# Eight pieces of a fused weight product put one by one in front of the forget-gate tiles, and a weight load moved behind the spreading of the reciprocals

## The chip, the cores and the metric

The kernel runs on one core of a Trainium2 chip. The metric is the device time of one execution in microseconds (us); before the change it is 2773.86 us, the median of 3 runs that lie between 2770.55 and 2777.31 us.

## The reference, cut to what matters

One decoder layer over 1024 tokens of width 1024, all in float32: two groups of 8 causal attention heads side by side (MLA, and FoX with a forget gate), an output projection, cross attention to 256 memory tokens with 4 heads, a mixture of 32 experts of which each token takes 4, and a last norm.

```
h = h + hybrid_mixer(rmsnorm(h, ln_mix), ...)
    # o_mla = causal_block_attention(q_mla, k_mla, v_mla, scale)
    # o_fox = causal_block_attention(fq, fk, fv, scale, c)   c: cumulative log forget gate,
    #         s = q @ k.T * scale + c[t] - c[s]; causal softmax; p @ v
    # return concat(rmsnorm(o_mla), rmsnorm(o_fox)) @ w_o
h = h + memory_cross_attention(rmsnorm(h, ln_cross), mem, ...)
    # k, v = split(rmsnorm(mem) @ w_mem_kv); p = softmax(q @ k.T * scale)
    # return concat over heads(p @ v) @ w_xo
h = h + moe_ffn(rmsnorm(h, ln_ffn), ...)
return rmsnorm(h, ln_final)
```

## The kernel before, in words

The program is written engine by engine: each engine has its own instruction list, run in the order in which it is written, and the lists meet at semaphores. The time has four big stages: projections (up to about 370 us), attention (370 to 705 us), cross attention and routing (to about 1130 us), experts (the rest). Only the attention stage is touched.

**The attention stage** runs over `HP` = 4 head pairs, called h = 0 to 3 here. The first three are iterations of a hardware loop, the fourth is written out behind it (`b_loop`). A head pair is two MLA heads and two FoX heads that share the row and column tiles. Inside one h there are `NP` = 16 positions p: p = 0 to 7 are the MLA tiles of 128 queries (y = 0), p = 8 to 15 the FoX tiles (y = 1, the "forget-gate pairs"). Tile i has 128·(i + 1) keys, and the order is `B_TILES = [6, 0, 7, 1, 5, 2, 4, 3]` in both halves, so p = 8 is tile 6, p = 9 tile 0, p = 10 tile 7, p = 11 tile 1, and so on. In each half every second tile is a short one (0, 1, 2, 3).

What happens to a tile, by engine and line:

- TensorE (PE) computes the scores into `wide[0]` and `wide[1]`, one for each of the two heads: `scores` (L1438) for MLA, `scores_pair` (L1455 and L1459) for FoX.
- VectorE (DVE) finds the lowest value of each row (L1950), for FoX it adds the forget-gate term first and puts the sum into `biased` (L1959).
- ScalarE (ACT) computes the exponential and the row sum (`b_exp`, L1109).
- PE turns the probabilities, 128 by 128 at a time (`turned`, L1312). DVE copies the first four blocks out of PSUM (L1970), ACT the rest (`b_second`, L1121).
- PE multiplies them with the values (`values`, L1494) into bank `pp[0]` or `pp[1]`, and ACT copies the result out (`b_out`, L1130).

PE works one tile ahead: at position p it turns tile p, computes the scores of tile p + 1, and multiplies the values of tile p - 1. At an odd FoX position the scores of p + 1 come first, at p = 8, 10, 12, 14 they come between the two heads' turns.

ACT's order at position p is `b_second(p, 0)`, `b_exp(p+1, 0)`, `b_second(p, 1)`, `b_exp(p+1, 1)`, `b_out(p-1)`, and then, where a head of the product below is complete, `mix_evict`.

**The fused product.** Beside the attention, each h computes a quarter (`MIX` = 256 columns) of (memory values) times `w_xo`, for the later cross attention. It is 8 pieces: 4 cross-attention heads `hd` by 2 blocks `mt` of 128 memory rows. A piece is `mixed(h, hd, mt, last)` (L1497 to L1507), two float32 products of 128x128 by 128x256; the trace shows a float32 product as two records of each kind. The two pieces of a head fill the two halves of one PSUM bank, `pp[1]`, which is the same bank that holds the values of p = 1, 3 and 5. So the first piece of each head waits until the bank is free, and the second tells ACT, which copies it out (`mix_evict`, L1142) and so frees it:

```
if mt == 0:
    pe.wait_ge(b_po[1].free, b_po[1].base + B_PO[1] * h + b_mix_use(hd))
    if hd == 0:
        pe.wait_ge(mix_in, mix_in_done + 16 * (h + 1))
```

`b_mix_use(hd)` counts the uses of the bank: 3 for values, then one per head. Hence the first piece of head 0 waits for `b_out(5)`, and that of head hd for `mix_evict(hd - 1)`. Where a piece stands is set by a table, `B_MIX`, whose rows are (position, hd, mt). PE puts the pieces of a position ahead of its turns:

```
if pair and y == 1 and not turn_first:
    scores_pair(*nxt)
for at_, hd, mt in B_MIX:
    if at_ == p:
        mixed(h, hd, mt, last)
for a_ in range(2):
    turned(h, p, a_)
```

`mix_evict(hd)` stands at the position of the second piece of its head.

**The loads and stores of the stage** are all issued by SyncE (SP) in one list for each h, `b_loads`: the MLA operands of the next h, the four stores of finished heads (`mix_store`, L661), the two spreads, the FoX operands of the next h (`load_fox`), and the next quarter of `w_xo` (`mix_load`, 1 MB into `mix_w`). A spread (`spread(h, y)`) takes the 16 rows of reciprocals of the softmax sums to a scratch tensor in HBM (`d_rr`, L676), waits for that store to land, and loads them back as `rr_all`, one row for 64 partitions. GpSimd (POOL) multiplies the output by it (`normalise`). For the last h, `mix_load` reads into `mix_w_last`, and the last third of `w_o` is loaded with it.

Of the kernel before, what the change touches and what calls it, by code (L numbers as in the profile page):

```python
# [78 lines left out]
def build(nc, S, a, out):  # L79
    T, D, NT, KD, H, FW, E, CAP = S.T, S.D, S.NT, S.KD, S.H, S.FW, S.E, S.CAP  # L80
    ctx = ExitStack()
    with ctx:
# [265 lines left out]

        B_MIX = [(NT + 2 * (n // S.MT), n // S.MT, n % S.MT) for n in range(S.XH * S.MT)]
        assert S.XH * S.MT * P == S.XH * S.M and B_MIX[-1][0] < NP - 1
        B_VALUES = [1 if p < NT - 1 and p % 2 else 0 for p in range(NP)]
        B_PO = [B_VALUES.count(0), B_VALUES.count(1) + S.XH]
# [219 lines left out]
        def rows(w):  # L574

            return w.rearrange("(k p) n -> p k n", p=P)
# [3 lines left out]
        def _(sp):  # L580
            def load(dst, src, s):
                sp.dma_start(dst, src).then_inc(s, 16)
# [64 lines left out]
            def load_mla(h):  # L647
                sp.wait_ge(b_in[0].free, h + 1)
                for dst, src in ((q_mla, d_q), (k_mla, d_k)):
                    load(dst[:, :, :], src[bass.ds(h * 2, 2), :, :].rearrange("h d t -> d h t"), b_in[0].full)  # L650

            def mix_load(h, last=False):
                if last:
                    sp.wait_ge(b_v, 2 * HP - 1)
                load(mix_w[last][:, :, :], rows(a["w_xo"][0])[:, :, bass.ds(h * MIX, MIX)], mix_in)

            def mix_store(h, hd, last=False):

                s = hd % 2
                sp.wait_ge(mix_full, mix_full_done + S.XH * h + hd + 1)  # L660
                sp.dma_start(d_vw[hd * S.M:(hd + 1) * S.M, bass.ds(h * MIX, MIX)].rearrange("(u m) n -> m u n", u=S.MT),  # L661
                             mix_out[last][s][:, :, :]).then_inc(mix_free[s], 16)

            def load_fox(h):
                sp.wait_ge(b_in[1].free, h + 1)
                for dst, src in ((q_fox, d_fq), (k_fox, d_fk)):
                    load(dst[:, :], src[bass.ds(h * P, P), :], b_in[1].full)
                sp.wait_ge(b_cneg.free, h + 1)
                for a_ in range(2):
                    load(cneg[a_][:, :], d_cneg[bass.ds(h * 2 + a_, 1), :].to_broadcast([P, T]), b_cneg.full)  # L670

            def spread(h, y):

                sp.wait_ge(b_row, 2 * h + y + 1)
                sp.wait_ge(b_all.free, 2 * h + y + 1)
                sp.dma_start(d_rr[y, :, :].rearrange("a (t p) -> (a t) p", p=P), rr_row[y][:, :]).then_inc(b_st, 16)  # L676
                sp.wait_ge(b_st, 16 * (2 * h + y + 1))
                for a_ in range(2):
                    load(rr_all[a_ * S.DV:(a_ + 1) * S.DV, :], d_rr[y, a_:a_ + 1, :].to_broadcast([S.DV, T]), b_all.full)
# [5 lines left out]
            def b_loads(h, last_mix):  # L685
                load_mla(h + 1)
                mix_store(h, 0)
                spread(h, 0)
                for hd in range(1, S.XH):
                    mix_store(h, hd)  # L690
                load_fox(h + 1)
                mix_load(h + 1, last_mix)
                if last_mix:
                    load(w_o[:, W_O_FIRST:, :], rows(a["w_o"][0])[:, W_O_FIRST:, :], ld["w_o"])
                spread(h, 1)

            with sp.Fori(0, HP - 2) as h:
                b_loads(h, False)
            b_loads(HP - 2, True)
            mix_store(HP - 1, 0, True)  # L700
            spread(HP - 1, 0)
# [312 lines left out]
        def _(ac):  # L1014
# [110 lines left out]
            def b_out(h, p):  # L1125

                (y, i), (b, use) = B_PAIRS[p], b_values_use(p)
                ac.wait_ge(b_po[b].full, b_po[b].base + B_PO[b] * h + use)
                apart(ac)
                ac.activation(o_t[:, bass.ds(h + y * HP, 1), i * P:(i + 1) * P].rearrange("p o t -> p (o t)"), pp[b][:, 0:P],  # L1130
                              ACT.Copy).then_inc(b_po[b].free, 1)
                ac.drain().then_inc(b_ot, 1)
# [13 lines left out]
            def b_body(h, last):  # L1146
                for p in range(NP):
# [5 lines left out]
                    if p:  # L1153
                        b_out(h, p - 1)
                    for at_, hd, mt in B_MIX:
                        if at_ == p and mt == S.MT - 1:
# [151 lines left out]
        def _(pe):  # L1308
# [134 lines left out]
            def scores_pair(h, p):  # L1443

                i = B_PAIRS[p][1]
                L = P * (i + 1)
                if p == NT:
                    pe.wait_ge(b_in[1].full, 32 * (h + 1))
                for a_ in range(2):
                    pe.wait_ge(b_s[a_].free, NP * h + p + 1)  # L1450
                half = [slice(a_ * S.DN, (a_ + 1) * S.DN) for a_ in range(2)]
                for c in range(0, L, 512):
                    w = min(512, L - c)
                    for a_ in range(2):
                        pe.matmul(wide[a_][:, c:c + w], q_fox[half[a_], i * P:(i + 1) * P], k_fox[half[a_], c:c + w],  # L1455
                                  start=True, stop=c + w < L)
                for idn, tri_mask, stop in ((ident_b, mask_b, False), (ident_x, mask_x, True)):
                    for a_ in range(2):
                        m = pe.matmul(wide[a_][:, L - P:L], idn[half[a_], :], tri_mask[half[a_], :], start=False, stop=stop)  # L1459
                        if stop:  # L1460
                            m.then_inc(b_s[a_].full, 1)
# [47 lines left out]
            def b_body(h, last):  # L1509
                for p in range(NP):  # L1510
# [4 lines left out]
# [4 lines that stand above are left out]
# [877 lines left out]
```

## Time and profile before

| what | value |
|---|---|
| time, median of 3 | 2773.86 us |
| the profiled execution's own time | 2772.76 us |
| its span in the profile | 2771.0 us |
| PE busy | 2663.8 us, 96% of the span |
| DVE, ACT, POOL busy | 39%, 23%, 14% of the span |
| mean granted TensorE clock | 0.986 |

The span is the stretch between the first and the last instruction of the profiled execution. In it PE is busy nearly all the time, and mostly in the experts. A busy share says nothing on one stage; for the attention stage it has to be read from that stretch.

### The profile page before, as it was taken

What the parts mean: (1) busy time and instruction counts of PE and PEld (TensorE: products, weight loads), DVE (VectorE), ACT (ScalarE), POOL (GpSimd) and SP (SyncE); (2) the same over time, 40 slices, a digit from 0 to 9 for tenths busy, and PEclk for the clock granted to TensorE, in tenths of its full rate; (3) what the DMA queues carried; (4) which work ended last, traced back from release to release, by engine and by line L of the source; (5) the groups of instructions that cost most, each with busy time, mean ns of one, the idle gap of its engine ahead of it and who ended that gap; (6) DMA issues with size and microseconds to landing.
All of it is one profiled execution on the core that took longest, in us unless ns stands there. A gap on an engine that the chain in (4) does not pass through costs nothing. (4 is left out here: it accounts for less than half of the span.)

```text
span 2771.0 us, 53372 instructions
## 1 busy us (share of the span) xinstructions
PE 2663.8 (96%) x19081; PEld 2288.0 (83%) x19082; DVE 1087.1 (39%) x2664; ACT 629.2 (23%) x1385; POOL 379.2 (14%) x390
## 2 busy tenths in 40 slices
PE   8999998899999999799999999999999999999997
PEld 7445556666458776699999999999999999999997
DVE  1111145455222323443333344344545454545454
ACT  0333344455001111011111111111212122121213
POOL 0000022112100000011111111111111111211112
PEclk9999999999999999899999999999999999999999
DMA  7111242322500000855666687787888888888785
GB/s 286 39 52 53 66 137 77 99 66 68 195 0 9 31 31 39 327 201 188 221 231 230 230 278 262 270 278 269 305 296 309 293 300 291 307 292 306 285 293 197
DMA packets 108867, 534.04 MB, mean 193 GB/s; under 512 B 24290, under 2 KB 59042, under 8 KB 84208
## 3 DMA queue, kind: packets, MB, share of 16 engines
q1 hardware_dynamic: 88016, 498.99, 49.2%
q0 software_dynamic: 20768, 33.97, 5.8%
q8 instruction: 49, 0.80, 0.1%
q14 instruction: 34, 0.28, 0.0%
HBM read 506.64 MB, written 60.52 MB: 205 GB/s over the span
## 5 line engine op out<-in xcount | busy, mean ns | idle before, releaser
L1319 PE MATMUL bank<-xe_t,slot 128*128 128x128 f32 (+4 forms) x8192 | 1022.4, 287 | 13.7 <-issue 12.5
L1319 PEld LDWEIGHTS bank<-xe_t,slot 128*128 128x128 f32 x8192 | 1013.0, 192 | 16.0 <-issue 15.9
L1734 PE MATMUL wide<-act_t,slot 128*128 128x128 f32 (+4 forms) x4096 | 513.3, 286 | 0.0
L1734 PEld LDWEIGHTS wide<-act_t,slot 128*128 128x128 f32 x4096 | 506.3, 191 | 0.0
L2235 DVE TENSOR_SCALAR glu<-bank,b_gu 128x256 f32<-128x256 f32 x256 | 123.9, 484 | 748.1 <-PE bank L1319 748.1
L1266 ACT ACTIVATE sig<-glu 128x256 f32<-128x256 f32 x256 | 106.6, 417 | 847.6 <-DVE glu L2235 844.0
L1373 PE MATMUL bank<-w_in,xt 128*128 128x512 f32 (+1 forms) x512 | 219.0, 581 | 3.8 <-DVEq L1878 3.8
L1277 ACT ACTIVATE y_t<-wide,b_dn 128x256 f32<-128x256 f32 x256 | 107.3, 470 | 427.4 <-PE wide L1734 427.4
L935 POOL DMA_INDIRECT xg<-d_xn,gidx x66 | 65.9, 999 | 900.9 <-DVEq L2194 890.9
L1373 PEld LDWEIGHTS bank<-w_in,xt 128*128 128x128 f32 x512 | 96.1, 193 | 104.1 <-issue 104.1
L948 POOL DMA_INDIRECT share<-d_gate,sidx x64 | 67.6, 1057 | 457.7 <-DVEq L2254 434.0
L2247 DVE TENSOR_TENSOR act_t<-lin,sig 128x256 f32<-128x256 f32 x256 | 108.9, 425 | 44.0 <-issue 11.2
L2237 DVE TENSOR_SCALAR lin<-bank,b_gu 128x256 f32<-128x256 f32 x256 | 121.7, 475 | 0.0
L1319 PEld LDWEIGHTS bank<-hn_t,w_xq 128*128 128x128 f32 x1024 | 115.5, 192 | 1.4 <-issue 1.1
L2244 DVE TENSOR_TENSOR lin<-lin,glu 128x256 f32<-128x256 f32 x256 | 108.8, 425 | 19.2
L1319 PE MATMUL bank<-hn_t,w_xq 128*128 128x128 f32 x1024 | 115.7, 275 | 0.3 <-issue 0.3
L1319 PE MATMUL wide<-vw,px_t 128*128 128x512 f32 x256 | 112.4, 593 | 0.6 <-DVE lg_now L2070 0.6
L1312 PE MATMUL bank<-const,prob 128*128 128x128 f32 x576 | 91.4, 288 | 21.6 <-ACT prob_t L1121 11.7
L958 POOL DMA_INDIRECT d_sum<-y_sb,sidx x62 | 100.7, 1624 | 39.1 <-ACTq L1247 24.2
L1837 DVE TENSOR_TENSOR xe_t<-bank,gains 128x512 f32<-128x512 f32 x132 | 85.3, 686 | 41.4 <-PE bank L1695 36.3
L1312 PEld LDWEIGHTS bank<-const,prob 128*128 128x128 f32 x576 | 64.4, 144 | 42.9 <-issue 15.6
L1970 DVE COPY prob_t<-bank 128x512 f32<-128x512 f32 (+3 forms) x128 | 75.7, 592 | 60.7 <-PE bank L1312 49.1
(282 smaller groups left out, 2321.2 us busy)
## 6 DMA issues: line engine op xcount, KB each, us to landing
slot<-in_w_gu SPq DMA_DIRECT2D x128, 2048.0 KB, 7.8
slot<-in_w_dn SPq DMA_DIRECT2D x64, 2048.0 KB, 7.7
w_in<-in_w_in SPq DMA_DIRECT2D x1, 6144.0 KB, 26.1
w_mem_k<-in_w_mem_kv SPq DMA_DIRECT2D x4, 1024.0 KB, 10.8
w_mem_v<-in_w_mem_kv SPq DMA_DIRECT2D x1, 4096.0 KB, 19.6
x_sb<-in_x SPq DMA_DIRECT2D x8, 512.0 KB, 3.3
cneg<-d_cneg SPq DMA_DIRECT2D x8, 512.0 KB, 6.9
d_vw<-mix_out SPq DMA_DIRECT2D x16, 256.0 KB, 2.2
```

The source lines that it names most:

```text
L958: po.indirect_dma_start(out=d_sum, out_offset=bass.IndirectOffsetOnAxis(ap=sidx[:, hb:hb + 1], axis=0), in_=y_sb[:, hb, :], in_offset=None ...
L1266: ac.activation(sig[m % 2][:, :], glu[m % 2][:, :], ACT.Sigmoid, scale=1.702).then_inc(e_sig, 1)
L1277: x = ac.activation(y_t[:, m, :], pp2[b][:, (m % 2) * CAP:(m % 2 + 1) * CAP], ACT.Identity, bias=b_dn[:, bass.ds(e * KD + m, 1)])
L1312: m = pe.transpose(dst[0:s.shape[-1], j * P:j * P + s.shape[0]], s, idn)
L1319: m = pe.matmul(dst, l, r_, start=(k == 0), stop=(k == n - 1))
L1373: m = pe.matmul(pp[b][:, 0:c1 - c0], xt[:, kk, :], w_in[:, kk, c0:c1], start=kk == 0, stop=kk == KD - 1)
L1734: x = pe.matmul(pp2[b][:, (m % 2) * CAP:(m % 2) * CAP + w], slots[4 + m // 4][:, k, (m % 4) * P:(m % 4 + 1) * P], act_t[:, k, 0:w], start= ...
L1837: return ve.tensor_tensor(dst, src.rearrange("p (k t) -> p k t", k=k), g.unsqueeze(2).to_broadcast([P, k, w]), ALU.mult)
L2235: ve.tensor_scalar(glu[b][:, :], pp[b][:, 0:CAP], b_gu[:, bass.ds(e * 2 * KD + 2 * m, 1)], 7.0, ALU.add, ALU.min).then_inc(e_glu, 1)
L2237: ve.tensor_scalar(lin[b][:, :], pp[b][:, CAP:2 * CAP], b_gu[:, bass.ds(e * 2 * KD + 2 * m + 1, 1)], 7.0, ALU.add, ALU.min).then_inc(e_gu[ ...
L2244: ve.tensor_tensor(lin[b][:, :], lin[b][:, :], glu[b][:, :], ALU.mult)
L2247: ve.tensor_tensor(act_t[:, m, :], lin[b][:, :], sig[b][:, :], ALU.mult).then_inc(e_act, 1)
```

## The change

Two edits. The table `B_MIX` had the two pieces of a head together, at p = 8, 10, 12 and 14. Now it has one piece at each position from 7 to 14: the first piece of a head at p = 7, 9, 11, 13, the second at p = 8, 10, 12, 14. The places at which ACT copies a head out stay. And in `b_loads`, `spread(h, 1)` goes ahead of `mix_load` and of the last part of `w_o`.

```
-        B_MIX = [(NT + 2 * (n // S.MT), n // S.MT, n % S.MT) for n in range(S.XH * S.MT)]
+        B_MIX = [(NT - 1 + n, n // S.MT, n % S.MT) for n in range(S.XH * S.MT)]
...
                 load_fox(h + 1)
+                spread(h, 1)
                 mix_load(h + 1, last_mix)
                 if last_mix:
                     load(w_o[:, W_O_FIRST:, :], rows(a["w_o"][0])[:, W_O_FIRST:, :], ld["w_o"])
-                spread(h, 1)
```

On PE, in the loop over h, at p = 7: the rows at L1494 are the values of p = 5, those at L1312 the turns of p = 7, and L1455 is the scores of p = 8.

```order
 L1494 MATMUL bank<-prob_t_125,v_now_134 64x128
 L1494 MATMUL bank<-prob_t_126,v_now_134 64x128
+L1500 REGISTER_ALU
+L1502 ISA
+L1319 MATMUL bank<-mix_w,vm_t 128x256 x2
 L1468 REGISTER_ALU
 L1312 MATMUL bank<-const,prob_119 128x128 x4
 L1312 MATMUL bank<-const,prob_120 128x128 x4
-L1448 ISA
+L1448 REGISTER_ALU
 L1450 REGISTER_ALU
 L1455 MATMUL wide<-k_fox,q_fox 128x512 x2
```

The first piece of head 0, with both of its waits, has moved in between the values of p = 5 and the turns of p = 7.

On PE at p = 11 and, below it, at p = 12 of the loop: L1459 ends the scores of p = 12, L1312 is the turns of p = 11, then L1494 is the values of p = 10, the last rows those of p = 12.

```order
 L1459 MATMUL wide<-mask_b,ident_b 128x128 x2
 L1459 MATMUL wide<-mask_x,ident_x 128x128 x2
+L1500 REGISTER_ALU
+L1319 MATMUL bank<-mix_w,vm_t 128x256 x2
 L1312 MATMUL bank<-const,prob_119 128x128 x2
 L1468 REGISTER_ALU
```

```order
 L1494 MATMUL bank<-prob_t_123,v_now_135 64x128
 L1494 MATMUL bank<-prob_t_124,v_now_135 64x128
-L1500 REGISTER_ALU
-L1319 MATMUL bank<-mix_w,vm_t 128x256 x4
+L1319 MATMUL bank<-mix_w,vm_t 128x256 x2
 L1312 MATMUL bank<-const,prob_119 128x128 x4
 L1468 REGISTER_ALU
```

The first piece of head 2, with its wait for the bank, now stands behind the scores of p = 12 and ahead of the turns of p = 11 and the values of p = 10; it stood behind these values. Positions 9 and 13 look the same.

On SP, at the end of one iteration of `b_loads`: the last load of FoX operands, then the quarter of weights and the spread.

```order
 L582 DMA cneg_139<-d_cneg 128x1024
-L582 ISA
-L582 DMA mix_w<-in_w_xo 128x8x256
 L674 REGISTER_ALU
 L676 DMA d_rr<-rr_row_131 16x128
 L677 REGISTER_ALU
 L582 DMA rr_all<-d_rr 64x1024 x2
+L582 ISA
+L582 DMA mix_w<-in_w_xo 128x8x256
```

The load of the weights has gone behind the store and the two loads of the spread.

## Rows read from the trace of the kernel before

**Rows 1.** Attention stage, busy us: PE, PEld, DVE, ACT, POOL; then clock, DMA, GB/s.

```profile
370.00:705.00 335.00, 302.09 (x2452) 210.61 (x2451) 177.56 (x336) 165.32 (x401) 71.13 (x39) 0.97 0.30 93
```

**Rows 2.** Timeline of PE, h = 0, p = 7 and 8: start us, us, instruction, [idle before].

```profile
403.30 0.66 PE L1312 MATMUL bank<-const,prob 128*128 128x128 f32 x4
404.47 0.66 PE L1312 MATMUL bank<-const,prob 128*128 128x128 f32 x4 [0.51 <-ACTq L1113]
405.06 1.77 PE L1455 MATMUL wide<-k_fox,q_fox 64*128 64x512 f32 x8
...
408.11 1.99 PE L1319 MATMUL bank<-mix_w,vm_t 128*128 128x256 f32 x8
409.94 0.93 PE L1312 MATMUL bank<-const,prob 128*128 128x128 f32 x7
```

**Rows 3.** Timeline of ACT, same stretch: the copy-out of p = 5, then exp(8, 0).

```profile
404.72 0.28 ACT L1130 ACTIVATE o_t<-bank 128x128 f32 x1 [0.34 <-issue]
...
409.48 0.19 ACT L1109 ACTIVATION_READ_ACCUMULATOR prob<-biased,low 128x1 f32 x1
```

**Rows 4.** Timeline of PE, h = 0: turns of p = 9, 11, 12 and 13.

```profile
416.80 0.44 PE L1312 MATMUL bank<-const,prob 128*128 128x128 f32 x2
...
425.71 0.66 PE L1312 MATMUL bank<-const,prob 128*128 128x128 f32 x4
...
430.02 0.82 PE L1312 MATMUL bank<-const,prob 128*128 128x128 f32 x6
...
435.00 0.87 PE L1312 MATMUL bank<-const,prob 128*128 128x128 f32 x6
```

**Rows 5.** Timeline of ACT, h = 0: heads 0, 1, 2 copied out; end of exp(12, 0).

```profile
415.68 0.60 ACT L1142 ACTIVATE mix_out<-bank 128x512 f32<-128x512 f32 x1 [0.35 <-issue]
...
426.47 0.60 ACT L1142 ACTIVATE mix_out<-bank 128x512 f32<-128x512 f32 x1 [0.34 <-issue]
...
428.17 0.19 ACT L1109 ACTIVATION_READ_ACCUMULATOR prob<-biased,low 128x1 f32 x1
...
435.81 0.60 ACT L1142 ACTIVATE mix_out<-bank 128x512 f32<-128x512 f32 x1 [0.35 <-issue]
```

**Rows 6.** Timeline, end of h = 0: a copy-out on ACT, and PE that waited for it.

```profile
451.30 0.28 ACT L1130 ACTIVATE o_t<-bank 128x128 f32 x1 [0.62 <-issue]
...
451.63 1.09 PE L1494 MATMUL bank<-prob_t,v_now 128*64 128x128 f32 x16 [1.87 <-ACT o_t L1130]
```

**Rows 7.** Timeline of PE, h = 3: turns of p = 7 and of p = 11.

```profile
654.05 0.66 PE L1312 MATMUL bank<-const,prob 128*128 128x128 f32 x4
...
676.29 0.66 PE L1312 MATMUL bank<-const,prob 128*128 128x128 f32 x4
```

**Rows 8.** Timeline of ACT, h = 3: copy-outs of p = 5 and of head 1.

```profile
655.22 0.28 ACT L1130 ACTIVATE o_t<-bank 128x128 f32<-128x128 f32 x1 [0.20 <-issue]
...
676.63 0.60 ACT L1142 ACTIVATE mix_out<-bank 128x512 f32<-128x512 f32 x1 [0.23 <-issue]
```

**Rows 9.** Timeline of SP's DMA issues at the turn from h = 0 to 1.

```profile
448.68 0.75 SPq L582 DMA_DIRECT2D mix_w<-in_w_xo  x1
450.24 1.54 SPq L676 DMA_DIRECT2D d_rr<-rr_row  x1
458.80 1.10 SPq L582 DMA_DIRECT2D rr_all<-d_rr  x2
```

**Rows 10.** Timeline of ACT: first turn-copy of h = 1 and of h = 3.

```profile
459.24 0.49 ACT L1121 ACTIVATE prob_t<-bank 128x384 f32<-128x384 f32 x1 [6.02 <-issue]
...
625.31 0.49 ACT L1121 ACTIVATE prob_t<-bank 128x384 f32<-128x384 f32 x1 [0.93 <-PE bank L1312]
```

**Rows 11.** DMA, 454 to 460 us: the queue that loads code; packets, MB, share.

```profile
q14 instruction: 3, 0.02, 1.0%
```

**Rows 12.** PE, h = 2 to 3: gap in the timeline; window with busy us, clock.

```profile
622.80 1.09 PE L1494 MATMUL bank<-prob_t,v_now 128*64 128x128 f32 x16 [1.86 <-ACT o_t L1130]
...
624.00:628.00 4.00, 4.00 (x22) 0.57 1.04 376
```

More of the change, by code:

```diff
@@ L347, in build @@
         B_ROWS = (NT, NP - 1)
-        B_MIX = [(NT + 2 * (n // S.MT), n // S.MT, n % S.MT) for n in range(S.XH * S.MT)]
+        B_MIX = [(NT - 1 + n, n // S.MT, n % S.MT) for n in range(S.XH * S.MT)]
         assert S.XH * S.MT * P == S.XH * S.M and B_MIX[-1][0] < NP - 1
@@ L691, in b_loads @@
                 load_fox(h + 1)
+                spread(h, 1)
                 mix_load(h + 1, last_mix)
@@ L694, in b_loads @@
                     load(w_o[:, W_O_FIRST:, :], rows(a["w_o"][0])[:, W_O_FIRST:, :], ld["w_o"])
-                spread(h, 1)
             with sp.Fori(0, HP - 2) as h:
```

## The prediction

> **What bounds the kernel now.** The change touches one stage, so the page's shares over the whole span are of no use, and I read the windows view of that stage first. In the 335 us of attention PE is busy 302 us, DVE 178 and ACT 165 [rows 1]. PE is the nearest thing to a bound, but it has 33 us of gaps, so this is a chain that goes round PE, DVE, ACT and back. What an insertion costs depends on whether PE is waiting at that place, and, new here, on whether the bank that the piece needs is free when PE gets there. So the next view is the timeline of PE beside that of ACT, position by position.
>
> At p = 7 PE goes from the values of p = 5 straight into the first turn at 403.30. It waits 0.51 us before the second, then issues the scores of p = 8 at 405.06 [rows 2]. At p = 8 the four products of head 0 start at 408.11 and the turns follow at 409.94, while the exponential they need ended at 409.48 + 0.19 = 409.67 [rows 2, 3]. There the old pair of pieces filled a wait almost exactly. At p = 12 it is different: the exponential was done at 428.36, and PE came to the turns at 430.02 [rows 4, 5]. From p = 9 on PE is the late one, and what delays it delays the stage.
>
> **The two edits, and what each costs.** No work is added or removed. PE runs the same 8 pieces for each h, ACT the same four copy-outs.
>
> *One piece.* Eight records start at 408.11 and the next work at 409.94, less a short start-up of the turns; I take 1.70 us for two pieces, 0.85 for one [rows 2]. Moving 0.85 us from behind the values to ahead of them costs nothing by itself where PE is busy throughout.
>
> *The wait that moves with the first piece.* It is for bank `pp[1]`. It used to be asked for well after the bank was free; now PE asks at an earlier point, and everything behind it on PE's list waits: the turns of the tile, the values, the next scores. I take 0.05 us from the end of a copy-out to PE's start, because a copy-out that ended at 451.30 + 0.28 = 451.58 let PE go at 451.63 [rows 6].
>
> - **p = 7, head 0.** The bank is freed by the copy-out of p = 5. ACT does that last in its round, after both exponentials of p = 7: 404.72 + 0.28 = 405.00 [rows 3]. PE is there at 403.30 [rows 2]. It waits until 405.05, does the piece until 405.90, then both turns without the old wait of 0.51. Two turns took 0.66 us or a little less each (404.47 to 405.06 is 0.59 [rows 2]); with 0.58 each the scores of p = 8 start at 407.06 in place of 405.06, 2.00 us late. DVE's `biased` and the exponential of p = 8 hang on these scores and on nothing else, so the turns of p = 8 can start about 0.05 after 411.67, against 409.81 to 409.94 before: 1.9 us late. The second piece, moved in behind 0.85 us of free room, does not matter there. For h = 3 the wait is 655.22 + 0.28 + 0.05 - 654.05 = 1.50 in place of 1.75 [rows 7, 8]; less that quarter, and the smaller wait that it saves, 1.75 us late.
> - **p = 9, head 1.** The scores of p = 10 now come before the piece and end at 416.80; head 0 was copied out at 415.68 + 0.60 = 416.28 [rows 4, 5]. The bank is free 0.5 us before PE asks. Cost 0, and what hides it are the long scores of tile 7; if they were 0.5 us shorter, the wait would show.
> - **p = 11, head 2.** The scores of p = 12 end at 425.71. Head 1 is copied out at 426.47 + 0.60 = 427.07, because ACT first does its copies and exponentials of that round [rows 4, 5]. PE waits 427.12 - 425.71 = 1.41 us. PE was the late one at p = 12 by 430.02 - 428.36 = 1.66 us, so nothing downstream swallows it: all of 1.41 goes on the path. For h = 3, where ACT's code has less to issue between instructions, it is 677.28 - 676.29 = 0.99 [rows 7, 8].
> - **p = 13, head 3.** The same: 435.81 + 0.60 + 0.05 - 435.00 = 1.46 us [rows 4, 5]. Both sides of this difference shift by the delays before it, so it stays. For h = 3 I take the 1.0 of p = 11 once more.
>
> One h of the loop: 1.9 + 1.41 + 1.46 = 4.8 us. The three iterations repeat each other within 0.05 us at the counterparts of these rows, so 3 x 4.8 = 14.3, and 1.75 + 0.99 + 1.0 = 3.7 for the last: **18.1 us**.
>
> Can it cost less? Where the pieces leave p = 10, 12 and 14 half empty, PE gets to the turns 0.85 us earlier than it would have, but it spent that 0.85 us two instructions before, so there is nothing to win; this is why I leave nothing for a gain.
>
> *The load behind the spread.* At the turn of h the store `d_rr` is issued at 450.24, behind `mix_w` at 448.68, and the loads that wait for it only at 458.80 [rows 9]: the tiny store landed with the megabyte ahead of it. In the new order the spread goes ahead, by something between 0 and the 8.6 us between those two issues. Who waits for it? POOL's `normalise`, and on that only the copy of the next reciprocals, half a head pair later. One head pair takes (654.05 - 403.30) / 3 = 83.6 us [rows 2, 7], so that is some 40 us. Nothing on the path. The weights come later by what the spread takes, at most another 8.6 us: before about 468. They are needed at p = 7 of the next h, at 403.3 + 83.6 = 487: 19 us to spare. If that cover were gone, PE would stand at p = 7 for the rest. Behind `mix_load` on SP's list stand the MLA operands of the h after, which wait for a buffer that is freed only at p = 6. Cost 0.
>
> There is one stall at this very place that could feel it. ACT does nothing for 6.02 us before the first copy of h = 1, but only 0.93 before that of h = 3, which is reached without a jump, with more data in flight [rows 10]. In these 6 us the queue that loads code moved 3 packets of 8 KB [rows 11]. I read this as ACT waiting for its own code after the jump back, in two or three steps of some 2 us, each about what a small store takes. The packets came also after the data had drained, at the same spacing, so I take 0 from the new order; bounds are -0.5 and +0.5 us for each of two jumps. The Trainium skill says under "Instruction fetch mechanics" in Runtime: NRT & Kernel Launch that a taken branch outside the loaded pages makes the engine wait for a DMA of the target page. By this rule the stall stays too, since both orders jump.
>
> **The sum.** The profiled execution took 2772.76 us, 1.1 below the median. 2772.76 + 18.1 = 2790.9; from the median, 2773.86 + 18.1 = **2792.0 us**.
>
> **The rivals.**
>
> 1. *The clock falls as well.* A gap of 1.86 us at the turn to h = 3 was followed by a clock of 0.57 in the mean of the next 4 us, at the lower of the two levels, 1.2 GHz, for most of them [rows 12]; an equal gap of 1.87 at the turn to h = 1 [rows 6] was not followed so at once. The new gap at p = 7 is 1.75 us, with 0.7 of idle again before the turns of p = 8. A mean of 0.57 over 4 us is 3.4 us at half rate, which costs at most 1.7 us. If it comes at each of the four gaps at p = 7, that is +7, 2799 us. Against it: part of that work lies in front of a wait, and the gaps of 1.4 are smaller. The Trainium skill says in TensorE: Matmul & The Clock Gate, Part 1, that idle time brings the clock to 1.2 GHz; a rule that speaks against every gap added, and the rows bear it out at one of two gaps of this size. One or two drops are within my range.
> 2. *Only p = 7 costs.* ACT might come to the copy-outs earlier when PE gives it fewer things to do, since the turns of p = 11 no longer compete. Then only 3 x 1.9 + 1.75 = 7.5 us remain: 2781. Against it: what precedes the copy-out on ACT comes from scores and turns that PE did before it reached the piece, and none of that moves.
> 3. *Faster: the jump.* If ACT's code waits behind the megabyte of weights in the DMA rings, the new order frees it, and the stall falls from 6.0 to the 0.9 of h = 3: -5.1 at two jumps, and the clock, which falls after the shorter gap of h = 3 too, might stay up, by the price of rival 1 another -1.7 each. That is -13.6 us against +18.1 for the pieces, so it decides only if the pieces cost under 13.6; with the 7.5 of rival 2 it would end 6 us below the time before, at 2768. For it: the stall and the load fall together at both jumps. Against it: h = 3 has the load and no stall.
> 4. *No difference.* Everything added is swallowed by the waits that follow; PE has 33 us of gaps in the stage [rows 1]. Against it: after p = 8 they do not lie behind the new waits.
>
> **How the numbers follow.** Forecast, with up to two clock drops: 0.74. Rival 1 in full: 0.10. Rival 2 or something between: 0.10. Rivals 3 and 4: 0.06 together, half of it faster. A difference below 0.2%, 5.5 us, could not be told from none here. Rival 2 at +7.5 is still slower. The likeliest case alone reaches from 2788 to 2797; to hold 8 in 10 I go from 2784 to 2799. Slower 0.93, same 0.04, faster 0.03.
>
> **What the new profile would show.** On PE, ahead of the first `mix_w` product of each h, 1.7 us idle put down to ACT's `o_t`; ahead of those of p = 11 and 13, 1.4 us put down to `mix_out`, 1.0 in h = 3; none at p = 9. The stretch from the first turn of p = 7 to that of p = 15 longer by 4.8. The wait of 6 us on ACT at both jumps unchanged, `rr_all` issued some us earlier, and every stage outside attention as long as before. The forecast is wrong if the gaps are there and the stage is not longer, or if ACT's stall at the jumps shrinks.

## The result, and the profile after

The changed kernel takes 2785.65 us, the median of 6 runs (2782.34 to 2788.96), against 2773.45 us (2770.55 to 2777.31, 6 runs). The ratio is 1.0045, 95% interval 1.0034 to 1.0056: it is slower by 12.5 us (9.4 to 15.5). The forecast was 2792.0 us, 18.1 us slower, in a range from 2784 to 2799. The measured time is in that range, 1.65 us above its lower end, and below the likeliest case alone, which was 2788 to 2797.

The first view is PE's timeline again, and of it the gaps: the pieces and the main gaps of h = 0, the row behind each of the two jumps, the last two pieces that waited in h = 3, and the first and last row of the stage. The columns are start, duration, instruction, and in brackets the idle time before it and what ended it. Changed kernel:

```profile
372.07 0.98 PE L1312 MATMUL bank<-const,prob 128*128 128x128 f32 x7 [0.84 <-ACTq L1113]
401.08 0.88 PE L1494 MATMUL bank<-prob_t,v_now 128*64 128x128 f32 x12
403.72 1.12 PE L1319 MATMUL bank<-mix_w,vm_t 128*128 128x256 f32 x4 [1.77 <-ACT o_t L1130]
405.65 1.77 PE L1455 MATMUL wide<-k_fox,q_fox 64*128 64x512 f32 x8
410.40 0.98 PE L1312 MATMUL bank<-const,prob 128*128 128x128 f32 x7 [0.57 <-ACTq L1113]
417.31 1.13 PE L1319 MATMUL bank<-mix_w,vm_t 128*128 128x256 f32 x4
427.62 1.13 PE L1319 MATMUL bank<-mix_w,vm_t 128*128 128x256 f32 x4 [1.34 <-ACT mix_out L1142]
438.42 1.13 PE L1319 MATMUL bank<-mix_w,vm_t 128*128 128x256 f32 x4 [1.39 <-ACT mix_out L1142]
447.54 1.07 PE L1312 MATMUL bank<-const,prob 128*128 128x128 f32 x8 [1.59 <-DVE prob_t L1970]
460.80 0.55 PE L1312 MATMUL bank<-const,prob 128*128 128x128 f32 x3 [1.36 <-ACT prob_t L1121]
...
533.97 1.07 PE L1312 MATMUL bank<-const,prob 128*128 128x128 f32 x8 [1.59 <-DVE prob_t L1970]
547.01 0.55 PE L1312 MATMUL bank<-const,prob 128*128 128x128 f32 x3 [2.35 <-ACT prob_t L1121]
...
686.35 1.13 PE L1319 MATMUL bank<-mix_w_last,vm_t 128*128 128x256 f32 x4 [0.92 <-ACT mix_out L1142]
696.75 1.13 PE L1319 MATMUL bank<-mix_w_last,vm_t 128*128 128x256 f32 x4 [1.00 <-ACT mix_out L1142]
710.63 7.13 PE L1319 MATMUL bank<-w_o,o_t 128*128 128x512 f32 x16 [0.72 <-ACTq L412]
```

The gaps are where they were forecast: 1.77 us at p = 7, put down to the copy-out of a value tile; no gap at p = 9 (417.31); 1.34 and 1.39 at p = 11 and 13, put down to the copy-out of a head; 0.92 and 1.00 in the last head pair. The waits of one kind summed over the stage:

```profile
PE bank L1319 <- ACT mix_out L1142: 10.1, 8, 1.4
PE bank L1319 <- ACT o_t L1130: 6.7, 4, 1.8
```

The columns are the total in us, the number of waits and the longest. That is 8 waits of together 10.1 us and 4 of together 6.7, which did not exist before. The surprise is on ACT, at the two jumps back in the loop. Answering to [rows 10]:

```profile
460.25 0.49 ACT L1121 ACTIVATE prob_t<-bank 128x384 f32<-128x384 f32 x1 [3.34 <-issue]
...
546.46 0.49 ACT L1121 ACTIVATE prob_t<-bank 128x384 f32<-128x384 f32 x1 [3.35 <-issue]
```

It stood still for 6.02 us there, now for 3.34 and 3.35. SP's issues at the turn, answering to [rows 9]:

```profile
453.71 0.33 SPq L676 DMA_DIRECT2D d_rr<-rr_row  x1
458.60 1.10 SPq L582 DMA_DIRECT2D rr_all<-d_rr  x2
459.90 0.43 SPq L582 DMA_DIRECT2D mix_w<-in_w_xo  x1
```

The loads of `rr_all` follow the store by 4.9 us in place of 8.6, and the weights are issued at 459.90, when ACT's wait, which ends at 460.25, is nearly over.

To see where time went I cut the stage at rows that exist in both traces. Two marks in each head pair are enough: the values of p = 5 (the last row that both kernels have ahead of the first new wait) and the turns of p = 15. The row of the changed kernel is 401.08 above; those of the kernel before:

```profile
373.48 0.98 PE L1312 MATMUL bank<-const,prob 128*128 128x128 f32 x7 [0.84 <-ACTq L1113]
402.50 0.88 PE L1494 MATMUL bank<-prob_t,v_now 128*64 128x128 f32 x12
444.06 1.06 PE L1312 MATMUL bank<-const,prob 128*128 128x128 f32 x8 [1.59 <-DVE prob_t L1970]
...
699.40 7.13 PE L1319 MATMUL bank<-w_o,o_t 128*128 128x512 f32 x16 [0.72 <-ACTq L412]
```

From the first turn to the first product with `w_o` the stage took 699.40 - 373.48 = 325.9 us before and 710.63 - 372.07 = 338.6 after: 12.6 us more. The *stretch of the pieces*, from the first mark to the second, took 444.06 - 402.50 = 41.56 us before and 447.54 - 401.08 = 46.46 after. It grew by 4.90, 4.88 and 4.86 us in the iterations of the loop and by 3.57 in the last head pair, 18.2 together. The *stretch of the jump*, from the second mark to the first one of the next head pair, shrank by 4.15, 0.76 and 0.65 us, 5.6 together. The third of these has no jump in it; there the clock fell in the kernel before (0.66 in the mean of the 5 us behind 622.80) and not in the changed one.

The 12.6 us are as much as the medians differ by. The two profiled executions differ by less, 9.6 us, because the rest of the program was 3.1 us shorter in the second: 1.4 ahead of the stage and 1.7 behind it, in code that is the same. I have no cause for that.

### The profile page after: what moved, and what is told of

It is laid out like the page before. It is cut to its first block and busy times, and to the rows that moved or that the text cites. A ratio compares the mean times of both kernels' runs of the same rounds, so it can differ in the third digit from the quotient of the medians.

```text
span 2780.5 us, 53372 instructions
## 1 busy us (share of the span) xinstructions
PE 2661.8 (96%) x19081; PEld 2283.4 (82%) x19082; DVE 1086.5 (39%) x2664; ACT 629.2 (23%) x1385; POOL 379.1 (14%) x390
## 5 line engine op out<-in xcount | busy, mean ns | idle before, releaser
L1319 PE MATMUL bank<-xe_t,slot 128*128 128x128 f32 (+4 forms) x8192 | 1022.4, 287 | 13.7 <-issue 12.5
L1312 PE MATMUL bank<-const,prob 128*128 128x128 f32 x576 | 88.3, 283 | 17.0 <-DVE prob_t L1970 7.1
L1312 PEld LDWEIGHTS bank<-const,prob 128*128 128x128 f32 x576 | 64.5, 142 | 39.2 <-issue 19.5
```

The source lines that it names most:

```text
L1312: m = pe.transpose(dst[0:s.shape[-1], j * P:j * P + s.shape[0]], s, idn)
L1319: m = pe.matmul(dst, l, r_, start=(k == 0), stop=(k == n - 1))
```

## The experiments

Eleven runs were made (e10 is the kernel of e6 once more), each timed beside the kernel before on the same chip. The last column is the attention stage in the profiled execution, from the first turn to the first product with `w_o`; in brackets the stall of ACT at the two jumps. The stage holds what the clock did around the jumps in that one execution; where this matters I use the stretch of the pieces, which repeats itself within 0.05 us from one iteration to the next.

| run | ratio to before (95%) | stage, us (stall, us) |
|---|---|---|
| before | 1 | 325.9 (6.02, 5.93) |
| after | 1.0045 (1.0034 to 1.0056) | 338.6 (3.34, 3.35) |
| e1: new table, old order | 1.0079 (1.0065 to 1.0093) | 348.8 (6.19, 5.93) |
| e2: old table, new order | 0.9987 (0.9978 to 0.9996) | 320.8 (3.33, 3.33) |
| e3: e2 and the piece at p = 7 | 1.0006 (0.9997 to 1.0015) | 331.8 (3.03, 3.38) |
| e4: e2 and the piece at p = 9 | 0.9978 (0.9969 to 0.9987) | 319.2 (3.31, 3.77) |
| e5: e2, half the weights ahead | 0.9991 (0.9981 to 1.0000) | 324.5 (5.08, 4.78) |
| e6: e2, head 3 at p = 15 | 0.9965 (0.9951 to 0.9979) | 318.9 (3.34, 3.49) |
| e7: after, copy-out first | 1.0035 (1.0021 to 1.0049) | 340.3 (3.98, 4.22) |
| e8: after, without p = 7 | 1.0019 (1.0010 to 1.0028) | 332.5 (3.42, 3.71) |
| e9: e6, FoX loads first | 0.9969 (0.9957 to 0.9981) | 318.4 (3.51, 3.00) |
| e10: e6 once more | 0.9966 (0.9954 to 0.9978) | 318.8 (3.58, 3.56) |
| e11: head 3 at p = 15, old order | 0.9960 (0.9947 to 0.9974) | 319.1 (4.00, 3.64) |

**The two edits apart.** e1 is the kernel before with the new `B_MIX` line alone, e2 the changed kernel with the old one:

```
-        B_MIX = [(NT - 1 + n, n // S.MT, n % S.MT) for n in range(S.XH * S.MT)]
+        B_MIX = [(NT + 2 * (n // S.MT), n // S.MT, n % S.MT) for n in range(S.XH * S.MT)]
```

Expected of e1:

> The new table of pieces with the old order of loads. Theory A (the bank waits cost what they were worked out to, and the new order of loads gives some back by shortening ScalarE's stall at the two jumps back): about +18 us, and the stall of ScalarE before the first turn-copy of h = 1 and h = 2 is 6 us, as before the change. Theory B (the pieces cost less than worked out, and the stall is shorter because they shift the moment of the jump against the loads): about +12 us, with the stall at 3.3 us as in the changed kernel.

Expected of e2:

> The old table with the spread ahead of the load of weights. Theory A: the stall falls from 6.0 to 3.3 us at both jumps and the time falls by 5 to 6 us, 0.2% faster than before. Theory B: the stall stays at 6 us and the time does not move, within 1.5 us.

Theory A stands. Of the two edits the stall goes with the order of the loads: 6.19 and 5.93 in e1, 3.33 twice in e2. The order alone makes the kernel faster by 0.13% (0.04 to 0.22), its stage by 5.1 us: 4.4 at the two jumps, and 0.7 in the stretch without a jump, where again the clock fell in the kernel before alone. And the new table on top of the new order costs 338.6 - 320.8 = 17.8 us in the stage, against 18.1 worked out. What I had not expected is that e1 costs more: 21.9 us by the ratio, 22.9 in the stage. Its trace shows why. Here are the windows of PE in e1 and, below them, around the same gap of the changed kernel (length, busy us with the number of records, granted clock, DMA share, GB/s):

```profile
402.00:405.00 3.00, 1.39 (x15) 1.00 0.15 12
405.00:410.00 5.00, 4.85 (x18) 0.66 0.93 236
497.00:502.00 5.00, 4.35 (x16) 0.66 0.95 232
589.00:594.00 5.00, 4.17 (x16) 0.66 0.90 226
```

```profile
400.57:403.57 3.00, 1.38 (x15) 1.00 0.02 7
403.57:408.57 5.00, 4.85 (x44) 1.00 0.95 237
```

The first two lines of each are cut at the same distance from the gap. In e1 the clock is at 0.66 in the mean of the 5 us behind the gap at p = 7 in all three iterations, that is for 3.4 us at the lower of the two levels, 1.2 GHz. In the changed kernel it stays at 2.4 GHz in all three, with the same gap, the same number of records and the same busy time ahead of it. What it cost, from the piece at p = 7 to the turns of p = 15:

```profile
405.15 1.45 PE L1319 MATMUL bank<-mix_w,vm_t 128*128 128x256 f32 x4 [1.77 <-ACT o_t L1130]
...
450.60 1.06 PE L1312 MATMUL bank<-const,prob 128*128 128x128 f32 x8 [1.59 <-DVE prob_t L1970]
```

450.60 - 405.15 = 45.45 us, against 447.54 - 403.72 = 43.82 in the changed kernel: 1.63 us for each fall, 4.9 for the three. So rival 1 is real, at its price of 1.7. Whether it comes is decided neither by the gap nor by the work around it, which are the same in both. e3 and e7 below have this gap too: the clock fell behind it in none of the three iterations of e3, as in the changed kernel, and in all three of e7, as in e1. What the DMA engines did in the 3 us up to the gap does not decide it either: their share was 0.05, 0.04 and 0.11 in e3, and 0.08, 0.05 and 0.19 in e7. I did not find out what does.

**The places apart.** e3 and e4 are e2 with one first piece moved, e8 is the changed kernel with one moved back:

```
+        B_MIX = [(p_, ...) for n, p_ in enumerate([7, 8, 10, 10, 12, 12, 14, 14])]   e3
+        B_MIX = [(p_, ...) for n, p_ in enumerate([8, 8, 9, 10, 12, 12, 14, 14])]    e4
+        B_MIX = [(p_, ...) for n, p_ in enumerate([8, 8, 9, 10, 11, 12, 13, 14])]    e8
```

> The new order of loads, and of the eight pieces only the first of head 0 moved ahead, to p = 7. Both theories agree on the mechanism here (TensorE waits 1.75 us for the copy-out of p = 5, 1.4 in h = 3) and differ in what it costs: by the working of the prediction 7.5 us above the run with the order alone; if the wait at p = 8 swallows part of it, 4 us or less.

> The new order of loads, and only the first piece of head 1 moved ahead, to p = 9, where the bank is free 0.5 us before it is asked for. By the bank-wait theory nothing: within 1 us of the run with the order alone. If it is the splitting of a head's two pieces itself that costs (one more change between kinds of products on TensorE), then 1.5 to 3 us more, a quarter of what the four splits cost.

> The changed kernel without its piece at p = 7: both pieces of head 0 at p = 8, the others one by one at p = 9 to 14. By the bank-wait theory the waits at p = 11 and 13 stay (1.4 us each, 1.0 in the last head pair) and the time is that of the order alone plus 10.5 us, about 2779, or 7.5 below the changed kernel. If the waits are not independent of each other, it lies elsewhere.

e3 is 0.19% above e2, 5.3 us; both intervals are some 2.5 us wide to a side, so 7.5 is within reach and 4 too. Its stage is 11.0 us longer. Of these, 7.2 lie in the stretches of the pieces (1.9 in each iteration, 1.45 in the last head pair; 7.5 worked out), and the rest at the jumps, where the clock fell more often; I don't charge that to the piece. e4 costs nothing: 0.9978 beside 0.9987, and its stretches of the pieces are those of e2 within 0.05 us. Splitting a head's pieces is free where the bank is free. e8 is 0.32% above e2, 8.9 us, its stage 11.7, its stretches 11.05, around the 10.5 worked out. The gaps in e8 are those of the changed kernel to the hundredth, 1.34 and 1.39. And the costs add up: in the stretches of the pieces p = 7 (e3) and the two later places (e8), measured apart, sum to 7.23 + 11.05 = 18.28 us over e2, and the changed kernel has 18.26 over e2. The waits are independent of one another. (The ratios, less sharp, give 14.2 apart and 16.1 together.)

**Taking the bank wait away.** In e7 ACT copies the head out at the start of its round, so that the bank is free before PE asks:

```
                     nxt = b_next(h, p, last)
+                    for at_, hd, mt in B_MIX:
+                        if at_ == p and mt == S.MT - 1:
+                            mix_evict(h, hd, last)
                     for a_ in range(2):
                         b_second(h, p, a_)
...
                         b_out(h, p - 1)
-                    for at_, hd, mt in B_MIX:
-                        if at_ == p and mt == S.MT - 1:
-                            mix_evict(h, hd, last)
```

> The changed kernel, with ScalarE copying a head out at the start of its round (ahead of both exponentials and of its copies of turned blocks) and not at the end. TensorE's waits for the bank at p = 11 and 13 (1.34 and 1.39 us) should be gone, the one at p = 7, which is for another copy-out, stays at 1.77. If these waits are on the path as worked out, up to 10.5 us come back; but the copy-out, with its issue 0.95 us, now stands ahead of the exponentials at four positions for each head pair, where ScalarE has no such room, up to 15 us more. Forecast between -6 and +4 us against the changed kernel; the waits tell, not the sum.

The waits summed over its stage:

```profile
PE bank L1312 <- ACT prob_t L1121: 14.9, 13, 2.5
PE bank L1319 <- ACT o_t L1130: 6.7, 4, 1.8
```

The line with `mix_out`, 10.1 us, is gone, and the waits for `prob_t` went from 6.6 us to 14.9. The two largest new ones in each head pair of the loop stand at the second head's turns of p = 8 and p = 10, where ACT now copies a head out ahead of the turned blocks:

```profile
415.26 0.55 PE L1312 MATMUL bank<-const,prob 128*128 128x128 f32 x3 [1.44 <-ACT prob_t L1121]
426.19 0.66 PE L1312 MATMUL bank<-const,prob 128*128 128x128 f32 x4 [1.00 <-ACT prob_t L1121]
```

The time is 1.0035, not told from the changed kernel, and the stretches of the pieces are the same in the loop, within 0.03 us, and 1.4 us shorter in the last head pair. But the clock was not the same. Two windows around the gap at p = 7 of e7:

```profile
400.25:403.25 3.00, 1.39 (x15) 1.00 0.08 10
403.25:408.25 5.00, 4.85 (x19) 0.66 0.96 238
```

It is at 0.66 behind this gap in all three iterations, and at 1.00 in the changed kernel. At the 1.63 us of e1 for each, copying out first gave back some 1.6 us for each head pair of the loop, out of the 2.73 that it took away in waits for the bank, and the clock took this again. So PE's wait was for the place of the copy-out on ACT's list, as stated; the earlier place costs a part of what it saves, not all of it. What e7 would take without the three falls was not measured.

**The stall at the jump.** In e5 half of the weights goes ahead of the spread:

```
                 load_fox(h + 1)
+                mix_load(h + 1, last_mix, (0,))
                 spread(h, 1)
-                mix_load(h + 1, last_mix)
+                mix_load(h + 1, last_mix, (1,))
```

> The old table; the quarter of weights is loaded in two halves of 512 KB, one ahead of the spread and one behind it. The two stalls of ScalarE were 6.0 us with the whole megabyte ahead and 3.3 us with none. If its code waits behind the data in flight, half the data gives about half the difference: 4.3 to 5.0 us at both jumps, and a time between those of before and of the order alone (2768.5 and 2772.5). If it is the order of the spread's small store that counts, and not the bytes, the stall is at one of the two old values.

```profile
458.53 0.49 ACT L1124 ACTIVATE prob_t<-bank 128x384 f32<-128x384 f32 x1 [5.08 <-issue]
...
543.51 0.49 ACT L1124 ACTIVATE prob_t<-bank 128x384 f32<-128x384 f32 x1 [4.78 <-issue]
```

The stall goes with the bytes of the weights ahead: 6.0 with 1 MB, 4.9 with half, 3.3 with none. The queue that loads code shows it from the other side. In the changed kernel, over 6 us around the stall:

```profile
q1 hardware_dynamic: 551, 1.05, 61.4%
q14 instruction: 3, 0.02, 1.6%
```

These are three packets, as in [rows 11]. But the third does not belong to the stall, neither here nor before: it comes when ACT is at work again. Read in windows of 0.1 us, the view of the DMA gives these moments, in us:

| kernel, jump | ACT idle | 1st packet | 2nd packet | ACT resumes | 3rd packet |
|---|---|---|---|---|---|
| before, 1st | from 453.2 | 454.6 | 457.4 | 459.24 | 459.7 |
| before, 2nd | from 538.9 | 540.7 | 543.0 | 544.84 | 545.3 |
| e5, 1st | from 453.4 | 455.3 | 456.7 | 458.53 | 460.2 |
| e5, 2nd | from 538.7 | 540.5 | 541.7 | 543.51 | 544.9 |
| after, 1st | from 456.9 | 457.7 | 458.0 | 460.25 | 461.6 |
| after, 2nd | from 543.1 | 543.9 | 544.4 | 546.46 | 547.9 |

From the start of the stall to the second packet it is 4.2 and 4.1 us before, 3.3 and 3.0 with half the weights ahead, 1.1 and 1.3 in the changed kernel. From the second packet to ACT's first instruction it is 1.8 to 2.2 us in all three. So the bulk data delays the packets, and the rest of the stall stays as it is. The profile does not say which engine's code a packet holds.

**Filling a gap in place of making one.** e6 moves both pieces of head 3 to p = 15, where PE waited 1.59 us for DVE and the bank was free:

```
+        B_MIX = [(p_, ...) for n, p_ in enumerate([8, 8, 10, 10, 12, 12, 15, 15])]
-        assert S.XH * S.MT * P == S.XH * S.M and B_MIX[-1][0] < NP - 1
+        assert S.XH * S.MT * P == S.XH * S.M and B_MIX[-1][0] < NP
```

> The new order of loads, the old table but for the two pieces of head 3, which go from p = 14 to p = 15, where TensorE sat idle 1.59 us ahead of its first turn while the bank of head 3 had long been free. If a piece costs its 0.85 us wherever TensorE is the late one and nothing in a gap, this gives 1.5 us for each of the four head pairs: 6 us less than the order alone, about 2762. What could take it back: the copy-out on ScalarE moves too, 0.95 us in front of the last copy-out of the head pair and of the jump; then 2 to 4 us less only, or nothing.

> The kernel with head 3 at p = 15 and the new order of loads once more, to stand beside the next one on the same chip: about 0.3% to 0.4% faster than before, 2763 to 2765 us.

e6 takes 2763.32 us, 0.35% less than before (0.21 to 0.49), and e10 confirms it with 0.34%. Against e2 that is 0.22%, 6.1 us, but with an uncertainty of 0.17%, 4.6 us, and the traces show half of it. The stage of e6 is only 1.9 us shorter than that of e2. Of the parts without a jump, the one from the values of p = 5 to those of p = 13 is shorter by 0.7 to 0.8 us in each head pair, and all of them together by 3.0. The gap of 1.59 at p = 15 is gone; the one behind it, ahead of values too, is now:

```profile
451.21 1.09 PE L1494 MATMUL bank<-prob_t,v_now 128*64 128x128 f32 x16 [1.58 <-ACT o_t L1130]
```

It was 1.87. What the sum of 1.5 for each head pair had left out is at p = 14. There the two pieces had covered waits of 0.75 us, which come out once they are gone:

```profile
438.11 0.66 PE L1312 MATMUL bank<-const,prob 128*128 128x128 f32 x4 [0.32 <-ACTq L1113]
439.19 0.33 PE L1312 MATMUL bank<-const,prob 128*128 128x128 f32 x1 [0.43 <-DVE prob_t L1970]
```

So the place at p = 15 is worth some 3 us by the traces, half of the expected 6. Two more kernels asked what part the loads have in this. e11 is e6 with the old order, e9 is e6 with this:

```
-                for hd in range(1, S.XH):
+                for hd in range(1, S.XH - 1):
                     mix_store(h, hd)
                 load_fox(h + 1)
+                mix_store(h, S.XH - 1)
```

> The kernel with head 3 at p = 15 and the spread ahead of the weights, and the FoX operands of the next head pair (2 MB written) loaded ahead of the store of head 3 and not behind it. That store waits for the last copy-out, so the loads should be issued some us earlier and be through before ScalarE jumps back. If the rest of the stall of 3.3 to 3.5 us at the jump is still waiting behind data, it falls to 2.5 or less and the time by 1 to 2 us against the same kernel without this. If 3.3 us is what a jump costs with the rings nearly empty, both stay.

> Head 3 at p = 15 with the old order of loads, one part of the faster kernel alone. If the two gains add up, this takes 6 us less than before by filling the gap of 1.59 us at p = 15 four times, about 2767, and ScalarE's stall stays at 6 us. If the copy-out in front of the jump takes the gain back when the weights are in flight, it is within 2 us of before.

e11 missed my expectation on one count: the stall did not stay at 6 us but fell to 4.00 and 3.64, and the kernel is not told from e6 and e10 (0.9960). SP's list explains it:

```profile
452.81 0.37 SPq L661 DMA_DIRECT2D d_vw<-mix_out  x1
453.38 0.37 SPq L582 DMA_DIRECT2D q_fox<-d_fq  x1
...
455.48 0.59 SPq L582 DMA_DIRECT2D mix_w<-in_w_xo  x1
```

The store of head 3 waits for its copy-out, which is now the last thing but one that ACT does ahead of the jump, and all loads stand behind the store. The stall begins at 453.24, a code packet passes at 455.1, and the megabyte is issued only at 455.48. With head 3 at p = 15 the order of the spread makes no difference that these runs can tell. e7 is the other side of it: it has the new order, but its loads come earlier, the weights are issued 1.1 us into the stall (457.82), ahead of the code packet at 458.9, and the stalls are 3.98 and 4.22. What counts is not the order on the list but what is in the DMA engines at that moment. And e9, which gets the 2 MB of FoX operands out of the way well before the jump, has stalls of 3.51 and 3.00 and is as fast as e10; from 442.9 us until 454.07, shortly ahead of the end of the stall at 454.54, only the 256 KB store of head 3 and the 8 KB of reciprocals are issued. So some 3.0 to 3.5 us is what a jump costs ACT here with little data in its way.

## Why the prediction was right, point by point

- **The pieces: right, in place and size.** Each of the three costs appeared with its releaser. The waits: 1.77, 1.34, 1.39 measured, 1.75, 1.41, 1.46 worked out. The stretch of the pieces grew by 4.9 in the loop (4.8 worked out) and by 3.6 in the last head pair (3.7 worked out). Sum 18.2 against 18.1. p = 9 cost nothing, as said, and e4 shows it alone. That the shortening at p = 10, 12 and 14 wins nothing was right too. In the sum for p = 7 two small errors cancel: a piece takes 0.96 us (403.72 to 404.68) and not 0.85, and the two turns behind it 0.97 and not 1.16, so that the scores of p = 8 are 2.0 us late, as worked out.
- **The load behind the spread: the step that failed.** "I take 0 from the new order; bounds are -0.5 and +0.5 us for each of two jumps." It is worth -2.7 and -2.6 us of stall, and -5.1 us in the stage (e2). The prediction's last line called it a sign of being wrong if ACT's stall at the jumps shrinks. It shrank, so on this edit the mechanism was wrong, and that the time still lies in the range is owed to the width of the range: without this term the sum is 5 to 6 us too high. The argument against rival 3 had three parts. That h = 3 has the load and no stall was right, but it shows only that without a jump there is no wait for code; it says nothing on how long the wait is where there is one. That the packets came at the same spacing after the data had drained was read from the third packet, which passed at 459.7, when ACT had been at work since 459.24. The two packets of the stall were 2.8 us apart while the data ran, and 0.3 in the changed kernel. And that both orders jump was right, and is why 3.3 us stay. Rival 3 was the right mechanism with the wrong size: not down to the 0.9 of a turn without a jump, but to 3.3.
- **Rival 1, the clock: right in price, and not settled in when.** It took 1.63 us for each fall in e1 and did not come at p = 7 in the profiled execution of the changed kernel. The prediction says that a fall followed one of two gaps of this size; the trace has a third, 1.86 us at the turn to h = 2 (537.32), with a clock of 0.65 in the 5 us behind it, so it was two of three. How much of the step from 2782.34, the profiled execution's own time, to the median of 2785.65 the clock explains was not measured. It points that way: the granted clock of that execution is 0.988 in the mean, and 0.986 or 0.987 in the other five, which took 1.9 to 6.6 us longer. At the jumps the clock also decided how much of the shorter stall arrived in the stage: the first stretch of the jump shrank by 4.15 us, the second by 0.76, with 2.7 and 2.6 us less stall. At the second, the lower level began as the score products began (they start at 547.98 and the first four records last 3.70 us), at the first it fell into the wait.
- **The cover of the weights: right.** They are issued at 459.90 and land some 6.3 us later. PE's first piece of h = 1 waits 1.76 us for `o_t` as in h = 0, and for nothing else.
- **Rivals 2 and 4** did not happen. Nothing was swallowed.

The sum that came out is 18.2 - 5.6 = 12.6 us.

## What to carry to other kernels

A piece of work that shares a PSUM bank with its own copy-out can't simply be spread thinner: look at when the reading engine gives the bank back, and place the next first piece behind that, because in an in-order list everything behind the piece waits too. Filler belongs where the engine idles and the bank is free; here the pieces of one head at p = 15 were worth some 3 us where eight spread pieces cost 18. Before a filler is moved out of a place, look for the wait that it covers there: it took back half of what was expected. And at a jump back in a hardware loop, keep bulk transfers out of the few microseconds in which an engine waits for its code.

## What the runs showed of the hardware that I had not expected

- ACT's wait after the jump back grew with the data ahead of its code in the DMA engines: 3.3 us with the weights behind, 4.9 with 512 KB ahead, 6.0 with 1 MB. In these three kernels the queue that loads code moved two packets of 8 KB during the wait. The Trainium skill says under "Instruction fetch mechanics" in Runtime: NRT & Kernel Launch that a taken branch outside the loaded pages forces a DMA fetch before execution goes on; the trace agrees, with 3.0 to 6.2 us behind every jump and 0.93 us, an ordinary wait for PE, where the same code follows without one. That this fetch shares the engines with bulk data and is delayed by it is what the runs add.
- With the same gap of 1.76 to 1.77 us ahead of the same piece the granted clock fell to 1.2 GHz in all three iterations of e1 and e7, and in none of the changed kernel and e3. Of the gaps of 1.86 to 1.87 us ahead of the values of p = 15, 11 of 27 were followed by a fall, in the nine kernels that have them; of those of 1.58 to 1.59 us none, in all thirteen traces.
